# Sparse attention in steps of two items: transposes one step behind, four score buffers, values of two heads on 64 columns each

## The chip, the cores and the metric

The kernel runs on one core of one Trainium2 chip. The metric is the device time of one execution in microseconds (us); three runs of the kernel before gave a median of 2213.21 us, from 2212.78 to 2218.43.

## The reference, cut to what matters

Two transformer blocks follow each other on a sequence of 256 tokens and a width of 1024. The second block has two layers; each mixes tokens by three branches (a convolution, a differential attention, a sparse attention), merges them by gates and adds a feed-forward part. The change lies in the sparse attention (`nsa_attention`) of these two layers: 8 heads of width 64 in two groups that share keys and values. With 256 tokens every block of keys is selected and the window covers all keys, so that both softmax branches are causal attention over 256 keys:

```python
o_cmp = jnp.einsum('bghsn,bngd->bsghd', p_cmp, vc_c)          # 15 compressed keys
o_sel = jnp.einsum('bqghn,bgqnd->bqghd', jax.nn.softmax(sc, axis=-1), vg)
o_win = jnp.einsum('bghqk,bkgd->bqghd', jax.nn.softmax(sc, axis=-1), vwin)
o = g[..., 0:1] * o_cmp + g[..., 1:2] * o_sel + g[..., 2:3] * o_win
...
merged = (gates[:, :, 0] * (y_a @ w_branch[0])
          + gates[:, :, 1] * (y_b @ w_branch[1])
          + gates[:, :, 2] * (y_c @ w_branch[2]))
```

## The kernel before

**Weights.** All weights come as one stream of 572 pieces (128x1024, 512 KB), loaded by SyncE into a ring of seven `raw` buffers. A dense product in about full precision is made of three fast ones: ScalarE rounds a piece to `whi` (L1113, `hi_to`), VectorE (L1721) or GpSimd (L2526) forms the rest `wlo` (`lo_to`), and TensorE adds `whi` times the high part, `whi` times the low part and `wlo` times the high part of the activations (`lin`, L464 to L466). `whi` and `wlo` are rings of five; `hi_to` and `lo_to` run four pieces ahead of their use, and the high part of a piece waits until TensorE has used the piece five before it. A tile of 128 outputs over 1024 inputs takes one piece and 24 products of 256 columns. The `raw` buffer of a piece is free once its low part is made.

**Order.** Every engine has its own function (`tensor`, `scalar`, `vector`, `gpsimd`), and each writes down its instructions in program order, which no scheduler changes. Waits are semaphores that the helper `on(point)` looks up. So a wait in one engine holds everything that stands behind it on that engine. Buffers and PSUM banks are rings: `bank("pm", ...)` hands out five banks in turn, `bank("pt", ...)` two, and `buf(...)` scratch buffers of `tmpb`; each request names the event until which the buffer is held.

**The stretch of the change.** In each layer, after the compressed keys are scored (`c_scores`, `c_turn`), a loop of 18 rounds interleaves the sparse attention with 18 dense tiles, `late(2)` to `late(19)`: the last two `ya` tiles (three pieces each) and 16 `gate` tiles (one piece each). The attention has 16 items, an item being one head and one half of the queries; `pair_item(n)` gives head `2*(n//4)+n%2` and half `(n//2)%2`. An item of half 0 sees 128 keys, one of half 1 sees 256. An item passes:

- `n_scores` (TensorE, L997, for two items at once): both branches, 64 rows of the array for each head;
- `masked` (VectorE, L2184 and L2187): mask, row maximum, its negative; per branch;
- exp with row sum (ScalarE, L1574), per branch;
- reciprocal, gate, scaling of the probabilities (VectorE, L2308, L2310, L2315);
- `n_turn` (TensorE, L1010): transposes, two for half 0 and four for half 1;
- copy of the transposes to `nT` (ScalarE, L1583).

`n_value(h)` (TensorE, L1020 to L1024) then multiplies values by probabilities for one head: compressed (15 rows), and for each branch 256 and 128 columns. The values `VD` and the compressed values `cmp_v` hold the 64 columns of a head twice side by side, so that the result stands on all 128 PSUM partitions; ScalarE (`YCh`, L1594) and VectorE (`YCl`, L2321) take the half that belongs to the head. The second copy in `VD` is made by VectorE (L2171, event `vdc`), and until then the PSUM banks of the values' projection are held.

In round n of the loop TensorE does: scores of n and n+1 if n is even, transposes of n-1, `late(n+2)`, values of the head that n-1 completed, and in four rounds `d_spread` for the other attention. VectorE does `masked(n)`, its part of `late(n+2)` (the low part of a weight piece), then the scaling of item n, then `YCl`. ScalarE does the exp of n, the copy of n-1's transposes, the high part of a piece and the activation of the gate (L1535), then `YCh`. The probabilities lie in a ring of three scratch buffers. After the loop comes the merge: for m in 0 to 7 a tile `mz` and three tiles `mb` (one for each branch, four input tiles each), the third of which reads `YCh` and `YCl`. ScalarE's gate of `mz` (L1616) goes to scratch buffers 3 and 4.

## Time and profile before

| | us |
|---|---|
| median of three runs | 2213.21 |
| lowest, highest | 2212.78, 2218.43 |
| the profiled execution, its time | 2212.25 |
| its span, first to last instruction | 2210.5 |
| TensorE busy | 2026.9 (92%) |
| VectorE busy | 1191.3 (54%) |
| ScalarE busy | 971.3 (44%) |
| GpSimd busy | 456.4 (21%) |
| loop of the change, layer 0: first scores to last values | 1239.2 to 1355.4 |
| the same in layer 1 | 1792.2 to 1904.5 |

Busy time of TensorE includes pipelined overlap, so that its stalls are better read from the waits and from gaps in its order of instructions. The mean granted clock of TensorE over the span is 0.953 of full speed; 1.00 is the level of 2.4 GHz and 0.5 that of 1.2 GHz, and a value between them is a stretch that had some of both.

### The profile page before, as it was taken

How to read it: one execution, taken by the hardware profiler on the slowest of the kernel's cores; microseconds unless marked ns; L12 is line 12 of the kernel's file. 1: busy time of each engine (PE TensorE's matmuls, PEld its weight loads, DVE VectorE, ACT ScalarE, POOL GpSimd, SP SyncE). 2: the span in 40 equal slices, each digit the busy share in tenths (PEclk: the TensorE clock that was granted, in tenths of full speed). 3: DMA queues.
4: the chain of work that ended last, by engine and by line, in shares of the span. 5: the costliest groups of instructions: out<-in, count | busy, mean ns of one | idle time of the engine just before them, and what ended most of it. 6: DMA issues, size and time to landing. Idle time of an engine off the chain costs nothing. (4 is left out here: it accounts for less than half of the span.)

```text
span 2210.5 us, 35650 instructions
## 1 busy us (share of the span) xinstructions
PE 2026.9 (92%) x14700; PEld 1788.8 (81%) x14700; DVE 1191.3 (54%) x2372; ACT 971.3 (44%) x1741; POOL 456.4 (21%) x247
## 2 busy tenths in 40 slices
PE   5999799999987998899998889999989889999997
PEld 2855578888866767799987879999988788899997
DVE  4787443233353554555565545664656555567464
ACT  3314432222333356444445444465544445446564
POOL 1030100000012135000001111435251111253534
PEclk8999899999997999999999999999999989999999
DMA  8234523223232342555533424545543342454551
GB/s 342 96 122 157 190 77 97 94 95 99 98 117 97 107 171 91 190 186 182 181 118 113 142 91 130 172 144 183 185 157 124 108 141 96 134 167 149 185 178 58
DMA packets 84546, 307.48 MB, mean 139 GB/s; under 512 B 9377, under 2 KB 10657, under 8 KB 84001
## 3 DMA queue, kind: packets, MB, share of 16 engines
q1 hardware_dynamic: 84384, 305.20, 41.3%
q8 instruction: 117, 1.92, 0.4%
q14 instruction: 45, 0.36, 0.1%
HBM read 304.12 MB, written 1.05 MB: 138 GB/s over the span
## 5 line engine op out<-in xcount | busy, mean ns | idle before, releaser
L464 PE MATMUL pb<-Hh,whi 128*128 128x256 f32 (+1 forms) x2832 | 890.0, 314 | 45.1 <-DVE Hl L1781 15.0
L465 PE MATMUL pb<-Hl,whi 128*128 128x256 f32 (+1 forms) x2832 | 878.8, 310 | 0.0
L466 PE MATMUL pb<-Hh,wlo 128*128 128x256 f32 (+1 forms) x2832 | 878.2, 310 | 0.0
L1721 DVE TENSOR_TENSOR wlo<-raw,whi 128x1024 fp32r<-128x1024 f32 x325 | 409.7, 1266 | 442.6 <-ACT whi L1113 442.0
L1113 ACT ACTIVATE whi<-raw 128x1024 fp32r<-128x1024 f32 x468 | 488.5, 1053 | 329.1 <-PE pb L466 317.2
L464 PEld LDWEIGHTS pb<-Hh,whi 128*128 128x128 f32 x2832 | 558.2, 197 | 73.8 <-issue 30.6
L465 PEld LDWEIGHTS pb<-Hl,whi 128*128 128x128 f32 x2832 | 558.4, 197 | 22.6
L466 PEld LDWEIGHTS pb<-Hh,wlo 128*128 128x128 f32 x2832 | 557.5, 197 | 23.1
L2526 POOL TENSOR_TENSOR wlo<-raw,whi 128x1024 fp32r<-128x1024 f32 x143 | 344.7, 2423 | 921.5 <-ACT whi L1113 921.5
L2534 POOL TENSOR_TENSOR X<-X,tmpb 128x512 f32<-128x512 f32 (+1 forms) x12 | 16.6, 1384 | 502.2 <-DVE tmpb L1822 502.2
L464 PE MATMUL pb<-hid_h,whi 128*128 128x512 f32 (+1 forms) x352 | 119.2, 339 | 0.0
L465 PE MATMUL pb<-hid_l,whi 128*128 128x512 f32 (+1 forms) x352 | 119.2, 339 | 0.0
L466 PE MATMUL pb<-hid_h,wlo 128*128 128x512 f32 (+1 forms) x352 | 119.2, 339 | 0.0
L464 PE MATMUL pb<-fh,whi 128*128 128x256 f32 x352 | 99.6, 283 | 0.0
L465 PE MATMUL pb<-fl,whi 128*128 128x256 f32 x352 | 99.0, 281 | 0.0
L466 PE MATMUL pb<-fh,wlo 128*128 128x256 f32 x352 | 99.0, 281 | 0.0
L514 PE MATMUL pb<-raw,csz 128*32 128x512 f32 x384 | 60.7, 708 | 26.4 <-DMA raw<-wstream 26.0
L1688 ACT ACTIVATE tmpb<-pb,VEC 128x256 f32<-128x256 f32 x88 | 48.4, 564 | 79.1 <-PE pb L466 79.1
L1867 DVE SCALAR_TENSOR_TENSOR Y<-U,VEC,Y 128x512 f32<-128x512 f32 x120 | 81.8, 755 | 0.0
L1275 ACT ACTIVATE tmpb<-pb 128x512 f32<-128x512 f32 (+1 forms) x44 | 21.6, 491 | 128.7 <-PE pb L466 128.7
L2486 DVE SCALAR_TENSOR_TENSOR tmpb<-pb,VEC,tmpb 128x255 f32<-128x255 f32 x88 | 42.4, 481 | 65.2 <-ACT tmpb L1688 64.1
L464 PEld LDWEIGHTS pb<-hid_h,whi 128*128 128x128 f32 x352 | 66.3, 188 | 8.0
(290 smaller groups left out, 2604.7 us busy)
## 6 DMA issues: line engine op xcount, KB each, us to landing
raw<-wstream SPq DMA_DIRECT2D x572, 512.0 KB, 3.5
X<-xin SPq DMA_DIRECT2D x2, 1024.0 KB, 8.4
CON<-consts SPq DMA_DIRECT2D x1, 1182.0 KB, 9.8
out<-X SPq DMA_DIRECT2D x8, 128.0 KB, 1.7
VEC<-vecs SPq DMA_DIRECT2D x1, 662.0 KB, 10.9
CON<-consts SPq DMA_DIRECT2D x1, 147.0 KB, 5.4
VEC<-vecs SPq DMA_DIRECT2D x1, 88.0 KB, 2.0
```

The source lines that it names most:

```text
L464: e.matmul(dst, hi, xh, start=k == 0, stop=False)
L465: e.matmul(dst, hi, xl, start=False, stop=False)
L466: i = e.matmul(dst, lo, xh, start=False, stop=k == kt - 1)
L514: i = e.matmul(dst[32 * c:32 * c + 32, :], csz[:, 4 * half + c, o:o + 32], raw[:, p % NRAW, (c % 2) * 512:(c % 2 + 1) * 512], start=m == h ...
L1113: e.activation(whi[:, s % NPIECE, :], raw[:, p % NRAW, :], ACT.Copy).then_inc(sig("act_hi", ("hi", p)), 1)
L1275: e.activation(t[:, 0:n], slots.at(("lin", "up", l, j, 0))[:, 0:n], ACT.Silu).then_inc(sig("act_ev", ("ev", "up", l, j, 0)), 1)
L1688: e.activation(t[:, s * T:(s + 1) * T], slots.at(("lin",) + key)[:, 0:T], ACT.Identity, scale=vec("ffn_conv_w_2", l * 132 + 88 + c), bias= ...
L1721: e.tensor_tensor(wlo[:, i, :], raw[:, p % NRAW, :], f32(whi[:, i, :]), ALU.subtract).then_inc(sig("dve_lo", ("lo", p)), 1)
L1867: c = e.scalar_tensor_tensor(out=y, in0=u, scalar=wt, in1=y, op0=ALU.mult, op1=ALU.add)
L2486: e.scalar_tensor_tensor(out=cv[:, 1:T], in0=bk[:, 0:T - 1], scalar=vec("ffn_conv_w_2", c + 44), in1=cv[:, 1:T], op0=ALU.mult, op1=ALU.add ...
L2526: e.tensor_tensor(wlo[:, i, :], raw[:, p % NRAW, :], f32(whi[:, i, :]), ALU.subtract).then_inc(sig("pool_lo", ("lo", p)), 1)
L2534: e.tensor_tensor(xs, xs, two(t) if segs == 2 else t[:, 0:T], ALU.add).then_inc(sig("pool_x", ("x", R, k)), 1)
```

## The change

The loop becomes nine steps of two items. In step P TensorE does the scores of items 2P and 2P+1, `late(2P+2)`, in steps 3, 5 and 7 the values of a pair of heads, the transposes of item 2P-2, `late(2P+3)`, the transposes of item 2P-1, and in steps 5 to 8 `d_spread`. The values of the last pair are computed after the first `mb` tile of the merge. VectorE masks both items of a step, scales item 2P, and scales item 2P+1 after its parts of both `late` tiles. The ring of probabilities gets a fourth buffer (scratch 7), and `nT` is held until the values of the pair. `VD` keeps the 64 columns once, VectorE's second copy and its event are gone, and the two heads of a pair are computed by products of 64 columns of weights, one on PSUM partitions 0 to 63 and one on 64 to 127, in turn. `YCh` and `YCl` are then one instruction for each pair.

```diff
-            scratch(11.5 + 10 * l, p=[0, 1, 2], nT=[3, 4, 5, 6, 9, 10])
+            scratch(11.5 + 10 * l, p=[0, 1, 2, 7], nT=[3, 4, 5, 6, 9, 10])
...
-                        lin_tok(key, "vvg", 280, 2, XS, xon, lambda s: [("vdc", l, s)])
+                        lin_tok(key, "vvg", 280, 2, XS, xon, lambda s: [("vda", l, s)])
...
-                    e.matmul(b[:, 0:T], cmp_v[g], PC[:, h, :], start=True, stop=False)
+                    halves = [(2 * hp + i, b[64 * i:64 * i + 64, 0:T]) for i in range(2)]
+                    for h, y in halves:
+                        e.matmul(y, cmp_v[h // 4][:, 0:64], PC[:, h, :], start=True, stop=False)
                     for br in range(2):
-                        a3 = two(slots.at(("nT", l, h, br)))
-                        e.matmul(b[:, 0:T], VD[:, 0, br, g, :], a3[:, 0, :], start=False, stop=False)
-                        i_ = e.matmul(b[:, 128:T], VD[:, 1, br, g, :], a3[:, 1, 128:T], start=False, stop=br == 1)
-                    i_.then_inc(sig("pe_att", ("no", l, h)), 1)
+                        for h, y in halves:
+                            e.matmul(y, VD[:, 0, br, h // 4, :], two(slots.at(("nT", l, h, br)))[:, 0, :], start=False, stop=False)
+                        for h, y in halves:
+                            i_ = e.matmul(y[:, 128:T], VD[:, 1, br, h // 4, :], two(slots.at(("nT", l, h, br)))[:, 1, 128:T],
+                                          start=False, stop=br == 1)
+                    i_.then_inc(sig("pe_att", ("no", l, hp)), 1)
...
-                for n in range(18):
-                    if n < 16 and n % 2 == 0:
-                        n_scores(n)
-                    if 0 <= n - 1 < 16:
-                        n_turn(n - 1)
-                    late(n + 2)
-                    if 0 <= n - 1 < 16 and pair_item(n - 1)[1]:
-                        n_value(pair_item(n - 1)[0])
...
+                for P in range(9):
+                    if P < 8:
+                        n_scores(2 * P)
+                    late(2 * P + 2)
+                    if P in (3, 5, 7):
+                        n_values((P - 3) // 2)
+                    if P:
+                        n_turn(2 * P - 2)
+                    late(2 * P + 3)
+                    if P:
+                        n_turn(2 * P - 1)
+                    if P > 4:
+                        d_spread(P - 5)
...
                         lin([("mb", l, m, br)], 4, src, T, xo)
+                        if m == br == 0:
+                            n_values(3)
...
+                for P in range(9):
+                    if P < 8:
+                        n_exp(2 * P)
+                    hi_to(("ya", l, 2, 0) if P == 0 else ("gate", l, LATE[2 * P + 2][1]))
+                    if P < 8:
+                        n_exp(2 * P + 1)
+                    late(2 * P + 2)
...
+                    if P in (3, 5, 7):
+                        yc_hi((P - 3) // 2)
+                    if P:
+                        n_out(2 * P - 2)
+                    late(2 * P + 3)
...
+                    if P:
+                        n_out(2 * P - 1)
...
-                            e.tensor_copy(VD[:, s, :, :, 64:128], b4).then_inc(sig("dve_cmp", ("vdc", l, s)), 1)
...
+                for P in range(9):
+                    if P < 8:
+                        n_masked(2 * P)
+                        n_masked(2 * P + 1)
+                    if P < 8:
+                        n_scaled(2 * P)
+                    late(2 * P + 2)
...
+                    if P in (3, 5, 7):
+                        yc_lo((P - 3) // 2)
+                    late(2 * P + 3)
...
+                    if P < 8:
+                        n_scaled(2 * P + 1)
```

TensorE at the values of the first heads, layer 0. Before, the values of head 0, then the next scores and the transposes of item 3, right before the next gate tile:

```order
L1020 MATMUL pb<-Y,MOD 128x256 [waits act_att,dve_ya]
L1023 MATMUL pb<-tmpb,VD 128x256
L1024 MATMUL pb<-tmpb,VD 128x128
L997 MATMUL pb<-KD,NQ 128x128 [waits dve_att]
L997 MATMUL pb<-KD,NQ 128x128 x3
L1010 MATMUL pb<-CON,tmpb 128x128 [waits dve_att]
L1010 MATMUL pb<-CON,tmpb 128x128 x3
L464 MATMUL pb<-Hh,whi 128x256 [waits dve_lo,act_ev]
```

Now, in step 3, the values of heads 0 and 1, two for two, and behind them the transposes of item 4, whose scores stood in step 2:

```order
L1022 MATMUL pb<-Y,MOD 64x256 [waits act_att,act_ev]
L1022 MATMUL pb<-Y,MOD 64x256
L1025 MATMUL pb<-tmpb,VD 64x256 x2
L1027 MATMUL pb<-tmpb,VD 64x128 x2
L1010 MATMUL pb<-CON,tmpb 128x128 [waits dve_att]
L1010 MATMUL pb<-CON,tmpb 128x128
L464 MATMUL pb<-Hh,whi 128x256 [waits dve_lo,act_ev]
```

(In both, the rows of the second branch, which repeat the first, are left away.) Ten products of 128 columns of weights for two heads have become ten of 64 columns, and what a transpose follows is no longer the scores of its own round.

ScalarE at the end of the loop and the first tile of the merge, layer 0. Before:

```order
L1535 ACTIVATE Y<-pb 128x256 [waits pe_lin]
L1594 ACTIVATE YCh<-pb 64x256 [waits pe_att]
L1599 ACTIVATE Hh<-DQ 128x256 [waits dve_ya]
L1113 ACTIVATE whi<-raw 128x1024 [waits raw_landed2]
L1535 ACTIVATE Y<-pb 128x256 [waits pe_lin]
L1113 ACTIVATE whi<-raw 128x1024 [waits raw_landed3]
L1616 ACTIVATE tmpb<-pb 128x256 [waits pe_lin]
L1113 ACTIVATE whi<-raw 128x1024 [waits raw_landed4]
```

Now:

```order
L1544 ACTIVATE Y<-pb 128x256 [waits pe_lin]
L1593 ACTIVATE tmpb<-pb 128x2x128 [waits pe_att]
L1593 ACTIVATE tmpb<-pb 128x2x128
L1622 ACTIVATE Hh<-DQ 128x256 [waits dve_ya]
L1122 ACTIVATE whi<-raw 128x1024 [waits raw_landed3]
L1639 ACTIVATE tmpb<-pb 128x256 [waits pe_lin,pe_att]
L1122 ACTIVATE whi<-raw 128x1024 [waits raw_landed4]
L1600 ACTIVATE YCh<-pb 128x256
```

The gate of `mz` (L1616, now L1639) has gained a wait for `pe_att`: its scratch buffer 3 holds `nT` of head 6 until the values of the last pair, which TensorE now computes after the first `mb` tile; `YCh` of that pair comes one piece later.

## Rows read from the trace of the kernel before

**Rows 1.** Page: span, and each engine's busy us (share) xinstructions.

```profile
span 2210.5 us, 35650 instructions
PE 2026.9 (92%) x14700; PEld 1788.8 (81%) x14700; DVE 1191.3 (54%) x2372; ACT 971.3 (44%) x1741; POOL 456.4 (21%) x247
```

**Rows 2.** Waits of TensorE: line waited by, for whom, us in total, times, longest.

```profile
PE pb L1010 <- DVE tmpb L2315: 32.7, 14, 5.1
PE pb L464 <- DVE VD L2171: 3.6, 2, 2.4
```

**Rows 3.** Timeline, rounds 6 and 7, layer 0: start us, us, [idle before <- releaser].

```profile
1287.79 1.13 PE L997 MATMUL pb<-KD,NQ 64*128 64x256 f32 x8
1288.86 0.44 PE L1010 MATMUL pb<-CON,tmpb 128*128 128x128 f32 x2
1289.06 0.42 DVE L2184 CUSTOM_DVE_ANT_0 tmpb<-pb,CON 128x256 f32<-128x256 f32 x1 [1.06 <-PE pb L997]
...
1290.76 0.43 ACT L1583 ACTIVATE tmpb<-pb 128x128 f32<-128x128 f32 x2
1291.07 1.06 ACT L1113 ACTIVATE whi<-raw 128x1024 fp32r<-128x1024 f32 x1
1292.16 1.23 DVE L1721 TENSOR_TENSOR wlo<-raw,whi 128x1024 fp32r<-128x1024 f32 x1 [1.95 <-ACT whi L1113]
1293.70 0.62 DVE L2315 TENSOR_SCALAR tmpb<-tmpb,SM 128x256 f32<-128x256 f32 x2
1294.46 0.41 PE L1010 MATMUL pb<-CON,tmpb 128*128 128x128 f32 x2 [2.29 <-DVE tmpb L2315]
```

**Rows 4.** Stretches of dense products: us, PE busy (x), PEclk, DMA share, GB/s.

```profile
1239.80:1248.70 8.90, 8.90 (x74) 1.00 0.18 58
1254.10:1264.40 10.30, 10.30 (x74) 0.83 0.45 144
1289.00:1292.10 3.10, 3.10 (x26) 1.00 0.01 1
1294.80:1299.40 4.60, 4.60 (x28) 0.63 0.25 97
```

**Rows 5.** Timeline of TensorE, values of head 0, layer 0, to the next scores.

```profile
1276.34 0.69 PE L1020 MATMUL pb<-Y,MOD 15*128 15x256 f32 x2
1276.96 0.70 PE L1023 MATMUL pb<-tmpb,VD 128*128 128x256 f32 x2
1277.50 0.38 PE L1024 MATMUL pb<-tmpb,VD 128*128 128x128 f32 x2
1277.72 0.60 PE L1023 MATMUL pb<-tmpb,VD 128*128 128x256 f32 x2
1278.15 0.39 PE L1024 MATMUL pb<-tmpb,VD 128*128 128x128 f32 x2
1278.47 0.38 PE L997 MATMUL pb<-KD,NQ 64*128 64x128 f32 x2
```

**Rows 6.** Timeline of TensorE, products on 32 columns; their line's loads, ns min/median/max.

```profile
19.45 1.07 PE L514 MATMUL pb<-raw,csz 128*32 128x512 f32 x8 [0.75 <-DMA raw<-wstream]
20.31 0.32 PE L554 MATMUL pb<-tmpb,CON 128*32 128x128 f32 x4
...
L514 PEld LDWEIGHTS pb<-raw,csz x384: 104/110/178, 6.2 to 896.1; 128*32 128x32 f32 x192
```

**Rows 7.** Timeline of VectorE, end of the values' projection, layer 0, and TensorE's next waits.

```profile
1178.29 2.81 DVE L1721 TENSOR_TENSOR wlo<-raw,whi 128x1024 fp32r<-128x1024 f32 x1 [0.48 <-ACT whi L1113]
1181.02 0.41 DVE L2171 COPY VD<-pb 128x256 f32<-128x256 f32 x1
...
1185.46 0.58 PE L546 MATMUL pb<-CON,tmpb 128*128 128x1 f32 x4 [0.72 <-ACT tmpb L1494]
```

**Rows 8.** Groups in the loop of layer 0: busy us, mean ns, idle before.

```profile
L1721 DVE TENSOR_TENSOR wlo<-raw,whi 128x1024 fp32r<-128x1024 f32 x14 | 18.2, 1303 | 29.9 <-ACT whi L1113 29.9
L1113 ACT ACTIVATE whi<-raw 128x1024 fp32r<-128x1024 f32 x21 | 22.1, 1055 | 1.6 <-PE pb L466 1.6
L1594 ACT ACTIVATE YCh<-pb 64x256 fp32r<-64x256 f32 x7 | 2.6, 378 | 12.2 <-PE pb L1024 12.2
```

**Rows 9.** Stretch of the loop, layer 0: us, PE, PEld, DVE, ACT, POOL busy, PEclk, DMA share, GB/s.

```profile
1239.20:1361.10 121.90, 105.04 (x760) 96.80 (x760) 59.49 (x206) 61.08 (x158) 19.06 (x8) 0.93 0.30 96
```

More of the change, by code:

```diff
@@ L1050, in tensor @@
                         else:
-                            src, xo = (lambda k: (YCh[:, k, :], YCl[:, k, :])), (lambda k: [("ycl", l, 2 * k), ("ycl", l, 2 * k + 1)])
+                            src, xo = (lambda k: (YCh[:, k, :], YCl[:, k, :])), (lambda k: [("ycl", l, k)])
                         lin([("mb", l, m, br)], 4, src, T, xo)
+                        if m == br == 0:
+                            n_values(3)
                 def centered(F, keys, kt, src, xo):
@@ new lines, in n_exp @@
+                def n_exp(n):
+                    nk = 128 * (pair_item(n)[1] + 1)
+                    p, sm = slots.at(("np", l, n)), slots.at(("nsm", l, n))
+                    for br in range(2):
+                        w.wait_ge(*on("nneg", l, n, br))
+                        pb = p[:, br * 256:br * 256 + nk]
+                        e.activation(pb, pb, ACT.Exp, bias=sm[:, 4 * br + 1:4 * br + 2], scale=SC,
+                                     accum_out=sm[:, 4 * br + 2:4 * br + 3]).then_inc(sig("act_att", ("nexp", l, n, br)), 1)
@@ new lines, in n_out @@
+                def n_out(n):
+                    h, qt = pair_item(n)
+                    if qt == 0:
+                        for br in range(2):
+                            for u in slots.take(st + 1.5, "nT", ("nT", l, h, br), ("no", l, h // 2)):
+                                w.wait_ge(*u)
+                    w.wait_ge(*on("nt", l, n))
+                    for br in range(2):
+                        i = e.activation(two(slots.at(("nT", l, h, br)))[:, 0:qt + 1, qt * 128:(qt + 1) * 128],
+                                         slots.at(("nt", l, n))[:, br * 256:br * 256 + 128 * (qt + 1)].rearrange(
+                                             "p (s q) -> p s q", q=128), ACT.Copy)
+                    i.then_inc(sig("act_att", ("nte", l, n)), 1)
@@ L1624, in scalar @@
                         hi_to(("mb", l, m, br))
+                        if m == br == 0:
+                            yc_hi(3)
                 merged(7)
@@ new lines, in n_masked @@
+                def n_masked(n):
+                    qt = pair_item(n)[1]
+                    nk = 128 * (qt + 1)
+                    p = buf(st + 1.5, "p", ("np", l, n), ("nt", l, n))
+                    sm = buf(0, "small", ("nsm", l, n), ("nn", l, n))
+                    w.wait_ge(*on("ns", l, n))
+                    for br in range(2):
+                        masked(slots.at(("ns", l, n))[:, br * 256:br * 256 + nk], nk, qt, p[:, br * 256:br * 256 + nk],
+                               sm[:, 4 * br:4 * br + 4], [("nmask", l, n)] if br else [], ("nneg", l, n, br))
@@ new lines, in n_scaled @@
+                def n_scaled(n):
+                    h, qt = pair_item(n)
+                    nk = 128 * (qt + 1)
+                    p, sm = slots.at(("np", l, n)), slots.at(("nsm", l, n))
+                    w.wait_ge(*on("nexp", l, n, 1))
+                    e.reciprocal(sm[:, 8:10], sm[:, 2:7:4]).then_inc(sig("dve_att", ("nrec", l, n)), 1)
+                    w.wait_ge(*on("nrec", l, n))
+                    e.tensor_tensor(sm[:, 10:12], sm[:, 8:10], gate3[:, qt, 3 * h + 1:3 * h + 3], ALU.mult).then_inc(
+                        sig("dve_att", ("ngate", l, n)), 1)
+                    w.wait_ge(*on("ngate", l, n))
+                    for br in range(2):
+                        pb = p[:, br * 256:br * 256 + nk]
+                        i = e.tensor_scalar(pb, pb, sm[:, 10 + br:11 + br], None, ALU.mult)
+                    i.then_inc(sig("dve_att", ("nn", l, n)), 1)
@@ new lines, in yc_lo @@
+                def yc_lo(hp):
+                    w.wait_ge(*on("ych", l, hp))
+                    e.tensor_tensor(YCl[:, hp, :], slots.at(("no", l, hp))[:, 0:T], f32(YCh[:, hp, :]), ALU.subtract).then_inc(
+                        sig("dve_ya", ("ycl", l, hp)), 1)
+                for P in range(9):
[5 more added lines that the diff above has]
+                    late(2 * P + 2)
+                    if P == 0:
+                        ya_lo(2, slots.at(("fa", l, 2))[:, 0:T])
+                    if P in (3, 5, 7):
+                        yc_lo((P - 3) // 2)
+                    late(2 * P + 3)
+                    if P == 0:
+                        ya_lo(3, slots.at(("fa", l, 3))[:, 0:T])
+                    if P < 8:
+                        n_scaled(2 * P + 1)
+                    if P > 5:
+                        ya_lo(P - 2, DQ[:, P - 6, :])
+                    if P > 4:
+                        w.wait_ge(*on("spread", ("d", l, P - 5)))
+                        e.scalar_tensor_tensor(out=DQ[:, P - 5, :], in0=DQ[:, P - 5, :], scalar=subln,
+                                               in1=slots.at(("spread", ("d", l, P - 5)))[:, 0:T],
+                                               op0=ALU.mult, op1=ALU.mult).then_inc(sig("dve_ya", ("dnorm", l, P - 5)), 1)
@@ L2333, in merged_lo @@
+                ya_lo(7, DQ[:, 3, :])
                 def merged_lo(k):
@@ L2344, in vector @@
                         lo_to(key)
+                        if m == br == 0:
+                            yc_lo(3)
                         gt = gate_at(8 * br + m) if br < 2 else slots.at(("g2", l, m))[:, 0:T]
```

96 lines of the change are left out of this document (16 added, 80 removed).

## The prediction

> **What bounds the kernel now.** The page first: TensorE is busy for 92% of the span, VectorE for 54%, ScalarE for 44% [rows 1]. So the end is set by TensorE, and the question of the change is where TensorE stands still, and what it does that it need not do. TensorE's list of waits answers the first part: its longest entry is the transpose of the sparse attention (L1010) behind VectorE's scaling (L2315), 32.7 us in 14 waits [rows 2]. They all lie in the two loops that the change rewrites. For the loop of layer 0 the windows give 105.04 us of TensorE in 121.9, thus 16.9 idle [rows 9], and the waits of that layer come to the same.
>
> The timeline shows why it waits. TensorE computes the scores of items 6 and 7 from 1287.79 and a gate tile to 1292.17, and can transpose item 6 only at 1294.46 [rows 3]. Between lie VectorE's mask (1289.06), ScalarE's exp, its copy of older transposes (1290.76), its high part of a weight piece (1291.07 to 1292.13), VectorE's low part of that piece (1292.16 to 1293.39) and only then the scaling (to 1294.32). The scaling stands behind the low part, the low part waits for the high part, and that stands behind the exp. The whole is 6.7 us, and TensorE has one round of work, some 4.4 us, to put beside it. No engine is full: they are in a ring, and the ring is shorter than its latency.
>
> A wait has an after-effect in the granted clock. Seventy-two dense products take 8.9 us at a clock of 1.00, and 10.3 us at 0.83 right behind the longest wait; twenty-four take 3.1 at 1.00 and 4.6 at 0.63 right behind a wait of 2.3 [rows 4]. These means are mixtures of the two levels, 1.2 and 2.4 GHz. Before each fall TensorE had stood still.
>
> **The change, part by part.** The sum is made against the profiled execution's own 2212.25 us, which is 1.0 below the median of the three runs shown.
>
> *Waits of the transposes.* A transpose of item 2P now stands a whole step behind its scores. A step of TensorE is scores (1.07 for two items of 256 keys [rows 3], less for 128), two tiles of 3.1 [rows 4] and two sets of transposes of some 0.2 to 0.4: 7.6 us at least. From the scores to the transpose of item 2P there are then that step, the next scores and a tile, 11 us or more, and 14 for item 2P+1. Against this: masks of two items (0.54 for each branch, from 1289.06 to 1289.60 [rows 3], so 2.2), the exp of some 1.1 for both branches, the scaling of 1.0 for item 2P, in all under 5; for item 2P+1 another high part of 1.06, two low parts of 1.3 [rows 8] and the scaling, in all under 10. Both fit with 4 us or more to spare, so I let all 32.7 us go.
>
> *The clock behind them.* In six of the 14 places the tiles behind ran slow: two times 1.4 (72 products) and four times 1.5 (24 products) [rows 4]: 8.8 us. No gap, no fall: -8.8.
>
> *Values on 64 columns.* A head costs 2.13 us (1276.34 to 1278.47) [rows 5]. From the same rows, a product of 256 columns takes 0.43 (1277.72 to 1278.15), one of 128 takes 0.22 (1277.50 to 1277.72): three and two of them are 1.73, and 0.40 is start and exposed weight loads. Sixteen heads are 34.1 us. Now two heads go together, half of the array's columns each. Whether the halves run at the same time the loop before doesn't show; the nearest row is L514, with 32 columns: eight instructions, which are four products of 512 columns on four column groups, start at 19.45 and the next line starts at 20.31 [rows 6]. That is 0.86 us for four, the time that one product of 512 columns takes by rows 5 (two times 0.43). So column groups overlap fully. For a pair the lower bound is 1.73, the upper one is no overlap and every load bare: 3.46 plus 20 loads of 0.11 [rows 6], 5.7. I take 1.73 plus the 0.40 of today plus 0.2 for entering and leaving another division of the array, 2.3, near the lower end because L514 is the same kind of product. Eight pairs are 18.4: -15.7, with bounds of -20.3 and +11.
>
> The Trainium skill (TensorE: Matmul & The Clock Gate, Part 3) speaks against this: it has weight loads overlap with running products only where the row groups differ, and the halves share all row groups. L514's groups share them too, and show no such cost in their 0.86 us; that rule's case is the second rival.
>
> *VectorE's second copy of the values.* TensorE waited 3.6 us in two places for it [rows 2], because it stood behind a low part that took 2.81 beside GpSimd [rows 7]. That wait goes, but not its whole price: TensorE next waits at L546 for ScalarE's square (0.72) [rows 7], whose chain starts on VectorE behind the same low part and moves up only by the two removed copies, 0.82. So 0.8 in layer 0 and some 1.3 in layer 1, whose wait was the longer: -2.1, with bounds of 0 and -5 (all of it and a slow tile).
>
> *Banks, buffers, the merge.* The fourth buffer of probabilities was the scratch of `ya` tile 2 and is free before item 3. The gate of the first `mz` on ScalarE now waits for the values of the last pair, which TensorE computes behind `mz` and an `mb` tile. ScalarE stands there some 6 us with four weight pieces, 12 us of TensorE, made ahead. After the values it does the gate (0.38), a high part (1.06) and `YCh` (0.38), then VectorE `YCl` (0.42): 2.2 us. TensorE has the second `mb` tile (1.5) and three of four inputs of the third (1.1) before it needs them, 2.6. I cost it at nothing; if the cover were 1 us short, it would be 2 us for both layers. Half of the `YCh` and `YCl` instructions go from engines that nobody waits for: nothing. The stream of weights: 96 GB/s in the loop [rows 9], a quarter faster after it, and 144 in a stretch of it [rows 4]: nothing.
>
> Sum: 2212.25 - 32.7 - 8.8 - 15.7 - 2.1 = 2152.95, and with the 1.0 to the median **2154 us**, 2.7% faster.
>
> **Rivals.**
>
> *Second: the halves don't overlap, or their loads stand bare.* A pair then costs 3.46 plus the 0.4 to 0.8 of starts, or 1.73 plus 20 loads of 0.11 plus some start, both about 4.1, as today. For it: a load of 64 columns has to happen between two products of the same half. Against it: L514. The time is 2154 + 8 x 1.8 = 2168.
>
> *Third: waits come back in another place.* For it: a low part took 2.81 instead of 1.23 where GpSimd worked beside it [rows 7], ScalarE and VectorE stand at `YCh` and `YCl` until the values are done (12.2 us before ScalarE's seven copies in layer 0 [rows 8]), and both keep strict order. Against it: of the new stretch, 121.9 less 16.9, 5.8 and 7.9, thus 91 us, VectorE's 59.5 and ScalarE's 61.1 us [rows 9] are two thirds. If half of the waits and slow tiles stay, it is 2154 + 20.7 = 2175.
>
> *Fourth, slower: the chain of a step does not fit into the next one.* ScalarE has the copy of item 2P-1's transposes, the last thing of TensorE's step, ahead of the next exp. If the exp starts so late that every scaling misses its transpose, all 32 transposes wait, not 14. At the 2.3 us of rows 3, with 1.5 us of slow clock in each of 16 steps, that is 98 us, and 2252 us. It decides against the change from a mean wait of 1.4 us on each transpose and those slow tiles, which use up the 59 us gained. Against it: the copy ends half a microsecond into the next step, and the exp's mask is ready only after 1.5 us.
>
> *Fifth: no change.* The wait of the transposes only showed the ring of weight pieces, and TensorE stands in front of its dense tiles instead, for the same time and with the same slow clock, the values saved being waited away too: 2213. Against it: no dense tile of the loop waited for a weight piece [rows 2, 8]; VectorE waited for ScalarE's high part (29.9 us) while TensorE was not waiting for VectorE's low part.
>
> **How the numbers follow.** Forecast 0.70, second 0.11, third 0.13, fourth 0.03, fifth 0.03. The range: below 2154 lie the bounds of the values (4.6), of the copy (3) and gaps whose hidden tail also goes, not all at once: 2146. Above, it takes in the second rival and the third as a whole: 2176. This leaves out the fourth and the fifth and ends below. Measured differences of 0.3%, 6.6 us, are about what can be told from no change for this kernel. The first three cases are faster than that, the fifth is the same: faster 0.94, same 0.03, slower 0.03.
>
> **What the profile of the changed kernel would show.** The entry L1010 behind VectorE's scaling gone from TensorE's waits, or under 2 us; no new entry there above 3 us in the two loops. A granted clock of 1.00 in both loops, and 0.96 to 0.97 over the span. From the first row of a pair's values to the next line 2.3 us; 4.1 would be the second rival. VD gone from the waits, and L546 waiting for ScalarE in both layers. `YCl` not among the waits of the merge. The loop of layer 0 in about 84 us instead of 116, its last values now behind it. Wrong would be the forecast if a dense tile (L464) or a set of transposes waits for VectorE or ScalarE in more than a few steps, which would show as gaps of 1 to 5 us with slow tiles behind them.

## The result, and the profile after

The changed kernel takes 2158.13 us (median of four runs, 2153.48 to 2165.93) against 2215.82 in the runs of the kernel before beside it: a ratio of 0.974, 95% interval 0.970 to 0.978, thus 2.6% faster. Its profiled execution took 2153.48, the one before 2212.25: 58.8 us less.

The page, span and busy times, to set beside [rows 1]:

```profile
span 2151.7 us, 35658 instructions
PE 2002.1 (93%) x14700; PEld 1767.0 (82%) x14700; DVE 1185.4 (55%) x2360; ACT 966.2 (45%) x1733; POOL 458.2 (21%) x247
```

TensorE's waits, to set beside [rows 2] (line waited by, for whom, us in total, times, longest):

```profile
PE pb L514 <- DMA raw<-wstream: 20.8, 10, 6.6
PE pb L546 <- ACT tmpb L1503: 3.7, 2, 2.2
PE pb L464 <- DVE YCl L2343: 0.8, 2, 0.4
```

L1010, with its 32.7 us, is no longer in the list at all. VD is gone, and L546 behind ScalarE has taken almost all of its place (3.7, before 0.7). `YCl` is new.

To compare kernels, take the stretch from the first sparse scores (L997) of a layer to the first product of the merge that reads `YCh`. It holds the same work in every kernel here: the attention, 18 tiles, one `mz` and two `mb` tiles, the values of all heads. I call it the loop stretch. Before, both layers (us, PE, PEld, DVE, ACT, POOL busy, PEclk, DMA share, GB/s):

```profile
1239.20:1364.10 124.90, 108.04 (x785) 99.80 (x785) 61.19 (x208) 62.40 (x160) 19.06 (x8) 0.93 0.31 99
1792.20:1913.24 121.04, 105.20 (x785) 96.93 (x785) 60.78 (x208) 62.39 (x160) 19.02 (x8) 0.96 0.32 103
```

and after, both layers:

```profile
1234.60:1327.70 93.10, 93.10 (x786) 86.11 (x785) 56.36 (x201) 59.37 (x156) 19.51 (x8) 1.00 0.42 138
1756.10:1849.20 93.10, 93.10 (x786) 86.13 (x786) 59.41 (x201) 59.55 (x156) 19.44 (x8) 1.00 0.42 137
```

In the changed kernel TensorE stands still in neither layer, and the clock is granted in full. Before, the two took 124.9 and 121.0, together 245.9; now 186.2. In the two stretches of before the clock was granted at 1.2 GHz in six places, 27.3 us in all, and TensorE was busy for 21.5 of them. The weights come at 138 GB/s now, before at 99, and no product in the stretch waits for them. The whole balance of the two profiled executions is then: loop stretches -59.7; all ahead of the first one -4.6 (1239.2 to 1234.6, with L514's waits for DMA 5.2 shorter); between them +0.3; behind the second +5.2. The sum is -58.8.

How far a transpose now stands from its scores, TensorE and VectorE, layer 0:

```profile
1277.29 0.71 PE L997 MATMUL pb<-KD,NQ 64*128 64x128 f32 x8
1280.12 0.48 DVE L2338 TENSOR_SCALAR tmpb<-tmpb,SM 128x128 f32<-128x128 f32 x2
1284.70 0.48 DVE L2338 TENSOR_SCALAR tmpb<-tmpb,SM 128x128 f32<-128x128 f32 x2
1290.90 0.44 PE L1010 MATMUL pb<-CON,tmpb 128*128 128x128 f32 x2
1294.05 0.38 PE L1010 MATMUL pb<-CON,tmpb 128*128 128x128 f32 x2
```

The scores of 1277.29 are scaled by 1280.6 and 1285.2 and transposed at 1290.90 and 1294.05: 9 to 10 us are to spare, where the transposes of [rows 3] waited 2.29. But this is the middle of the loop. The least is near its start, at item 3 of layer 0 (its scaling, and the transposes that read it):

```profile
1264.99 0.62 DVE L2338 TENSOR_SCALAR tmpb<-tmpb,SM 128x256 f32<-128x256 f32 x2
1267.14 0.60 PE L1010 MATMUL pb<-CON,tmpb 128*128 128x128 f32 x4
```

Between the end of the scaling, 1265.6, and the transposes lie 1.5 us. Items 1 and 2 have 1.6 and 2.5 there, the same three items of layer 1 have 2.2, 3.1 and 4.3, and every other item has 5.9 or more. In VectorE's order the scaling of item 1 stands behind its parts of both `ya` tiles, three weight pieces each, and items 2 and 3 stand behind that.

### The profile page after: what moved, and what is told of

Same layout as the page of the kernel before. It is cut to its first block, busy times and chain, and to the rows that moved or that the text cites. A ratio compares the mean times of both kernels' runs of the same rounds, so it can differ in the third digit from the quotient of the medians.

```text
span 2151.7 us, 35658 instructions
## 1 busy us (share of the span) xinstructions
PE 2002.1 (93%) x14700; PEld 1767.0 (82%) x14700; DVE 1185.4 (55%) x2360; ACT 966.2 (45%) x1733; POOL 458.2 (21%) x247
## 4 chain that ended last, share of the span: by engine, by line
PE 84%; DVE 9%; ACT 4%; DMA 1%; issue 1%; POOL 0%; ACTq 0%; SPq 0%; DVEq 0%
PE pb L464 24%; PE pb L465 23%; PE pb L466 23%; DVE Y L1892 2%; DVE wlo L1746 1%; DMA raw<-wstream 1%; PE pb L514 1%; ACT whi L1122 1%; DVE tmpb L2435 1%; PE pb L722 1%; PE pb L782 1%; PE pb L864 1%; PE pb L571 1%; PE pb L997 1%; PE pb L1010 1%
## 5 line engine op out<-in xcount | busy, mean ns | idle before, releaser
L514 PE MATMUL pb<-raw,csz 128*32 128x512 f32 x384 | 60.6, 708 | 21.2 <-DMA raw<-wstream 20.8
L466 PEld LDWEIGHTS pb<-hid_h,wlo 128*128 128x128 f32 x352 | 66.2, 188 | 8.0
```

The costliest lines, as they stand in the source:

```text
L466: i = e.matmul(dst, lo, xh, start=False, stop=k == kt - 1)
L514: i = e.matmul(dst[32 * c:32 * c + 32, :], csz[:, 4 * half + c, o:o + 32], raw[:, p % NRAW, (c % 2) * 512:(c % 2 + 1) * 512], start=m == h ...
```

## The experiments

Times are medians with the lowest and highest run; the ratio is to the kernel before in the same job (medians 2213.78, 2212.88, 2213.92 and 2216.46). "Loops" is the sum of the two loop stretches in the profile.

| kernel | median us | ratio, 95% interval | loops us |
|---|---|---|---|
| before | 2215.82 | 1 | 245.9 |
| lag alone | 2196.12 (2189.77-2201.23) | 0.992 (0.989-0.995) | 224.7 |
| pair values alone | 2203.27 (2199.36-2212.79) | 0.995 (0.993-0.997) | 232.3 |
| lag and pair values, rounds of one | 2186.99 (2185.11-2191.33) | 0.989 (0.985-0.992) | 212.6 |
| steps of two, values close | 2171.13 (2167.83-2178.45) | 0.982 (0.978-0.986) | 198.3 |
| changed | 2158.13, again 2161.45 | 0.974, 0.975 (0.972-0.977) | 186.2, 186.2 |
| changed, no lag | 2185.03 (2182.06-2188.36) | 0.987 (0.984-0.990) | 214.4 |
| changed, 128-column values | 2181.37 (2176.59-2184.26) | 0.985 (0.982-0.988) | 202.7 |
| changed, halves in turn | 2180.77 (2175.20-2184.69) | 0.984 (0.981-0.988) | 202.1 |
| changed, three buffers | 2158.57 (2151.14-2165.63) | 0.973 (0.969-0.978) | 186.3 |
| changed, copy put back | 2155.28 (2151.74-2161.63) | 0.973 (0.970-0.977) | 186.1 |
| changed, gates moved | 2161.93, again 2157.37 | 0.975, 0.974 (0.972-0.977) | 186.1, 186.1 |

**The lag alone.** The kernel before with transposes, copies and values one item further behind, and the fourth buffer:

```diff
-                    if 0 <= n - 1 < 16:
-                        n_turn(n - 1)
+                    if 0 <= n - 2 < 16:
+                        n_turn(n - 2)
```

> The kernel before, with the transposes (and all that follows them) two items behind the scores instead of one, and the fourth buffer; rounds, values on 128 columns and the second copy as before. If the lateness of the scaling was all that the transposes waited for, the 32.7 us of waits at L1010 and the 8.8 us of slow tiles go: about 2171 us on the profiled run, 0.981 of before. If the grouping in steps of two was needed as well, waits of 10 us or more stay at L1010: 2185 or more.

The loops lost 21.2 us, not 41.5. Neither half of the expectation fits: the time is that of the second, 2185 or more, but the waits that it names, at L1010, are not there. L1010's wait for the scaling is down to 0.8 us, as it should be, but two waits have come in (TensorE's waits of this kernel):

```profile
PE pb L1020 <- ACT tmpb L1583: 7.7, 4, 3.1
PE pb L464 <- DVE SM L2184: 5.2, 3, 2.7
```

The values wait for ScalarE's copy of the transposes, although a dense tile lies between, and a dense tile waits for VectorE's mask, until which the scores hold a PSUM bank. This is my third rival, in a kernel that has only a part of the change.

**The pair's values alone.** The kernel before with 64-column values and no second copy, its lag of one item kept:

```diff
-                    if 0 <= n - 1 < 16 and pair_item(n - 1)[1]:
-                        n_value(pair_item(n - 1)[0])
+                    if 0 <= n - 1 < 16 and n % 4 == 0:
+                        n_values(n // 4 - 1)
```

> The kernel before, with the values of a pair of heads on 64 columns each and without the second copy; rounds and lag as before. If the terms simply add, 17 to 19 us go: 2195. If the ring of mask, exp, weight piece and scaling sets the pace of the loop (four rounds in 23.0 us), the values were hidden beside it and TensorE waits longer at its transposes instead: L1010 waits of 40 us or more, and a gain of 2 to 6 us only, 2206 to 2210.

The loops lost 13.6 us, so the gain lies between the two expectations. A part of what TensorE saved it stood waiting, with three more waits and 2.4 us more than in [rows 2], and not the 40 us or more of the second:

```profile
PE pb L1010 <- DVE tmpb L2314: 35.1, 17, 5.1
```

**Values on 128 columns in the changed kernel** (two banks for a pair, VectorE's second copy back):

```diff
-                    halves = [(2 * hp + i, b[64 * i:64 * i + 64, 0:T]) for i in range(2)]
-                    for h, y in halves:
-                        e.matmul(y, cmp_v[h // 4][:, 0:64], PC[:, h, :], start=True, stop=False)
+                    for i in range(2):
+                        h, y = 2 * hp + i, bs[i][:, 0:T]
+                        e.matmul(y, cmp_v[h // 4], PC[:, h, :], start=True, stop=False)
```

> The kernel after, with the values of each head on 128 columns again, one head after the other in two banks, and with the second copy and its wait. If TensorE is now the bound of the loops, the whole difference of the values comes back, 8 times 4.26 less 2.03 us, 17.8, and 1 us for the copy: 19 us above the kernel after, about 2172 on a run like its profiled one. If something else paces the loops, less than 8 us.

The loops grew by 16.5 us, about the 17.8 expected. A pair took 4.17 us (1277.93 to 1282.10) in place of 2.03. The median is 23 us above the changed kernel's, where 19 were expected, and so is the profiled span. Of these 23, 6.1 us lie ahead of the first scores (1240.8 against 1234.6), where the same code differs from profile to profile (below).

**The changed kernel without the lag**, transposes in the step of their scores. The values of a pair then stand in steps 2, 4, 6 and 8 (the lines shown are those of the transposes):

```diff
-                    if P:
-                        n_turn(2 * P - 2)
+                    if P < 8:
+                        n_turn(2 * P)
```

> The kernel after, with the transposes of items 2P and 2P+1 in step P itself, behind the first and the second dense tile, and the values in steps 2, 4, 6 and 8. If the lag of a step is what removes the waits, they come back as before, 25 us or more at L1010 with slow tiles, 2185 or more. If the order of a step (both masks first, scaling of item 2P ahead of the weight pieces) does most of it, by the durations only items 2P+1 of odd steps wait, some 1 us each: 5 to 12 us of waits, 2160 to 2166.

```profile
PE pb L1010 <- DVE tmpb L2334: 19.3, 11, 5.7
```

The loops grew by 28.2 us, of which 19.3 are this wait (and 1.5 for ScalarE). A part of the rest is slow clock: right behind the wait of 5.69 us the eight products of the next scores took 2.08 us, in [rows 3] 1.13. TensorE was busy for 10.1 us at 1.2 GHz in the two loops, which costs half of that, 5.0; the last 2.4 us are not accounted for. The time is that of the first expectation, but the waits lie between the two: the order in steps takes 13.4 of the 32.7 us away without the lag. The lag is the largest single edit: 21.2 us as the first part; as the last 28.2, together with the values' other place.

**Halves in turn.** The five products of one head, then the five of the other, same shapes and same columns:

```diff
                     for h, y in halves:
                         e.matmul(y, cmp_v[h // 4][:, 0:64], PC[:, h, :], start=True, stop=False)
-                    for br in range(2):
-                        for h, y in halves:
+                        for br in range(2):
```

> The changed kernel with one edit: of a pair's ten products the five of the first head come first, then the five of the second, in place of one and one. The shapes, the columns used and the waits stay. If the two halves of the array run beside each other only because neighbours in the queue use different halves, a pair goes from the 2.03 us of the changed kernel's trace (1271.80 to 1273.83) to 3.5 to 4.1: 1.73 for each head, or the 4.1 of my second rival. Eight pairs are then 12 to 16 us, and the time 2170 to 2174. If it is enough that both are in the queue, or if a product of 64 columns is cheaper for another reason, a pair stays at 2.0 to 2.5 and the time within 4 us of the changed kernel's.

TensorE's timeline of a pair in the changed kernel, to the next transposes:

```profile
1271.80 0.65 PE L1022 MATMUL pb<-Y,MOD 15*64 15x256 f32 x4
1272.38 0.65 PE L1025 MATMUL pb<-tmpb,VD 128*64 128x256 f32 x4
1272.86 0.39 PE L1027 MATMUL pb<-tmpb,VD 128*64 128x128 f32 x4
1273.08 0.60 PE L1025 MATMUL pb<-tmpb,VD 128*64 128x256 f32 x4
1273.51 0.39 PE L1027 MATMUL pb<-tmpb,VD 128*64 128x128 f32 x4
1273.83 0.44 PE L1010 MATMUL pb<-CON,tmpb 128*128 128x128 f32 x2
```

and with the halves in turn, the first head and the start of the second:

```profile
1278.05 0.64 PE L1022 MATMUL pb<-Y,MOD 15*64 15x256 f32 x2
1278.62 0.65 PE L1024 MATMUL pb<-tmpb,VD 128*64 128x256 f32 x2
1279.10 0.38 PE L1025 MATMUL pb<-tmpb,VD 128*64 128x128 f32 x2
1279.32 0.59 PE L1024 MATMUL pb<-tmpb,VD 128*64 128x256 f32 x2
1279.75 0.38 PE L1025 MATMUL pb<-tmpb,VD 128*64 128x128 f32 x2
1280.07 0.64 PE L1022 MATMUL pb<-Y,MOD 15*64 15x256 f32 x2
```

A product is two instructions here, each with its weight load. Each row of the first view has four instructions in the time in which the second has two. A pair goes from 2.03 to 4.03 us (1278.05 to 1282.08), and the loops grow by 15.9, eight times 2.0. The gain of the shape comes from the alternation: a product of 64 columns is hardly cheaper than one of 128 (a head takes 2.02 here, 2.13 in [rows 5]), and no product of the second head starts ahead of the first head's. It isn't the loads that alternation hides. They are hidden with the halves in turn as well. Weight loads of this kernel, the first head's:

```profile
1278.62 0.19 PEld L1024 LDWEIGHTS pb<-tmpb,VD 128*64 128x64 f32 x2 [0.38 <-issue]
1278.89 0.35 PEld L1025 LDWEIGHTS pb<-tmpb,VD 128*64 128x64 f32 x2
```

The first load starts with its own product; the next ones run beside products of the same half, which last from 1278.62 to 1279.27. What alternation gains is that the products of the two halves run side by side.

The time is not the 2170 to 2174 expected but 2180.77: in the profile, 6.3 us more than in the changed kernel's stand ahead of the first scores, 5.6 between the two loop stretches, and 1.4 fewer behind the second.

**Three buffers** of probabilities in the changed kernel:

```diff
-            scratch(11.5 + 10 * l, p=[0, 1, 2, 7], nT=[3, 4, 5, 6, 9, 10])
+            scratch(11.5 + 10 * l, p=[0, 1, 2], nT=[3, 4, 5, 6, 9, 10])
```

> The changed kernel with three buffers of probabilities in place of four. The masks of item n then wait until item n-3 has been transposed: those of 2P+1 for the transpose of 2P-2, which TensorE does in the same step behind a dense tile. Theory A (there is slack enough): from that transpose to the one of 2P+1 are a dense tile, another step's scores, a tile and a set, 10 us or more, against masks, exp and scaling of about 3.5; the time stays within 4 us of the changed kernel's and no wait on VectorE's scaling over 1 us returns. Theory B (the fourth buffer is what makes the lag work): the waiting masks hold VectorE's low parts behind them, as it keeps strict order, so dense tiles (L464) or transposes (L1010) wait, 1 to 2.3 us in most of eight steps of two loops, with slow tiles: 2175 to 2200.

Theory A. The loops are the same to 0.1 us, and no wait for the scaling came back. In this order the fourth buffer does nothing.

**The copy put back** (VectorE writes the values once more, and TensorE waits for it):

```diff
+                            e.tensor_copy(VD[:, s, :, :, :], slots.at(("lin", key, s))[:, 0:256].rearrange(
+                                "p (b g d) -> p b g d", b=2, g=2)).then_inc(sig("dve_cmp", ("vdc", l, s)), 1)
```

> The changed kernel with VectorE's second copy of the values put back (it writes again what ScalarE wrote), and the values waiting for it. My sum had 2.1 us for the copy. If that holds: a wait of about 1.2 us on VD in each layer in TensorE's list, the wait of L546 on ScalarE falls from 3.7 in two places to 0.7 in one, and the profiled time is 0 to 3 us above the changed kernel's. If the copy costs nothing because L546 waits for the same chain anyway: VD and L546 together come to the 3.7 us of now. If it costs more, up to 5, a further slow tile stands behind the wait. The runs' times alone can't tell these apart; the waits can.

```profile
PE pb L464 <- DVE VD L2195: 3.6, 2, 2.4
...
PE pb L546 <- ACT tmpb L1503: 0.7, 1, 0.7
```

VD and L546 come to 4.3 us with the copy and to 3.7 without it. In the waits the copy is worth 0.6 us, less than any run can tell. Whether a slow tile hangs on it stays open: between the two loop stretches, where the second of these waits lies, this profile took 433.4 us and the changed kernel's 428.4, but kernels without the copy have 433 to 434 there too (values close, halves in turn).

**The gates' scratch moved** to buffers that the attention leaves earlier, so that ScalarE's first gate of the merge doesn't wait for the last values:

```diff
-            scratch(12 + 10 * l, mg=[0, 1, 2], g2=[3, 4])
+            scratch(12 + 10 * l, mg=[0, 1, 2], g2=[9, 10])
```

> The changed kernel with the two scratch buffers of the merge's gates moved to numbers 9 and 10, which the attention leaves earlier, so that ScalarE's first gate need not wait for the values of the last pair. Its only trace in the changed kernel is TensorE's wait of 0.40 us in each layer for the last YCl. My theory: ScalarE does the gate and its high parts ahead, YCh and YCl come some 0.4 to 0.8 us sooner, both waits go, 0.8 us in all, which the runs' times can't tell from nothing. Rival: the gate is held by something else (its own accumulator or the order of VectorE), and the waits stay at 0.3 to 0.5 each.

Both waits for `YCl` went, as expected, and 914.1 us from the first scores to the end stood against 917.1. To settle it, both kernels ran again in one job:

> The changed kernel as it is, once more, beside the one with the gates' scratch moved. From the first sparse scores of layer 0 to the end its profile should have 917 us within 1, as it had (917.1), and so had the kernels with three buffers (916.7) and with the copy put back (917.3). The start before these scores, which no part of the change touches, was 1232.6 to 1250.6 us in the profiles so far: if that is what spreads the runs over 2151 to 2166, a longer profile of this kernel has its excess there and nowhere else.

> The changed kernel with the gates' scratch moved, once more and in the same job as the changed kernel itself, to settle whether it is the better version. From the first sparse scores to the end its first profile had 914.1 against 917.1, with both waits for YCl gone. If that is real: 914 to 915 again, 2 to 3 us below the changed kernel's, and a median lower by 0 to 3, which 5 rounds can hardly tell. If it is an accident of the clock: 916 to 918 for both and no order in the medians.

From the first scores to the end the changed kernel had 917.0, the one with the gates moved 917.0 as well. Its waits for `YCl` are gone in both profiles, and the time is not lower: medians 2161.93 and 2157.37 against 2158.13 and 2161.45. No version here beats the changed kernel measurably. The second expectation, that a longer profile has all its excess ahead of the first scores, came true: 2158.7 against 2151.7 us of span, and 1241.7 against 1234.6 at the scores.

**Lag and pair values, rounds of one item.** The two parts together, in the order of the kernel before:

```diff
-                        n_turn(n - 1)
+                        n_turn(n - 2)
...
-                    if 0 <= n - 1 < 16 and pair_item(n - 1)[1]:
-                        n_value(pair_item(n - 1)[0])
+                    if 0 <= n - 2 < 16 and n % 4 == 1:
+                        n_values(n // 4 - 1)
```

> The kernel before with three parts of the change and without the fourth: transposes two items behind, four buffers, the 64-column values of a pair; but in rounds of one item, and the values right behind the round that made the last transposes. Counted from the first sparse scores of layer 0 to the end, which leaves out the start, the profiles so far give 971.3 us before, 955.3 with the lag alone, 960.6 with the pair's values alone, 917.1 with the whole change: 16.0 and 10.7 apart, 54.2 together, so 27.5 us belong to neither part alone. Theory A (lag and 64 columns help each other: each hides in the other's wait): this kernel has most of the 27.5 us, thus 917 to 925, a time of 2158 to 2168, and no waits over 1 us in the loops. Theory B (the order in steps with the values a scores and a tile later is what is missing): the waits of the lag alone remain, values on ScalarE's copy 7.7 us and dense tiles on the mask 5.2 us, each with slow tiles behind; 971.3 less 26.7, about 945, a time near 2185.

Theory B, in size (2186.99, and 947.3 us from the first scores to the end) and in the waits:

```profile
PE pb L1021 <- ACT tmpb L1586: 9.7, 6, 3.2
PE pb L464 <- DVE SM L2183: 5.0, 2, 2.7
PE pb L1010 <- DVE tmpb L2314: 2.4, 3, 1.2
```

The 27.5 us that belong to neither part alone are not something that the two parts give each other. In the loops they gave 21.2 and 13.6 alone and 33.3 together, and from the first scores to the end 16.0 and 10.7 alone and 24.0 together: by either sum they about add up. What is left belongs to the order in steps, 26.4 us in the loops. The timeline shows how rounds of one item make the wait (VectorE, ScalarE, TensorE, layer 0):

```profile
1281.47 1.23 DVE L1722 TENSOR_TENSOR wlo<-raw,whi 128x1024 fp32r<-128x1024 f32 x1 [2.05 <-ACT whi L1116]
1283.40 0.29 DVE L2183 CUSTOM_DVE_ANT_0 tmpb<-pb,CON 128x128 f32<-128x128 f32 x1
1283.92 0.40 ACT L1577 ACTIVATE tmpb<-tmpb,SM 128x128 f32<-128x128 f32 x1 [2.21 <-DVE SM L2186]
1284.71 0.64 ACT L1586 ACTIVATE tmpb<-pb 128x256 f32<-128x256 f32 x2
1285.49 1.12 PE L1021 MATMUL pb<-Y,MOD 15*64 15x256 f32 x4 [3.21 <-ACT tmpb L1586]
```

The scores of two items are made together (1272.03), but the odd one is masked only a round later, behind a low part (1281.47) and a scaling. ScalarE stands 2.21 us in front of its exp, with the copy of older transposes behind it, and for that copy TensorE waits 3.21, although a dense tile stands between these transposes and the values. A step of two masks both items ahead of the low parts.

**Steps of two, values close.** The changed kernel, a pair's values right behind its last transposes. The last pair's values move from the merge into step 8:

```diff
-                    if P in (3, 5, 7):
-                        n_values((P - 3) // 2)
...
+                    if P in (2, 4, 6, 8):
+                        n_values(P // 2 - 1)
```

> The changed kernel with a pair's values moved back to the end of the step that makes its last transposes, ahead of the next scores, so that ScalarE's copy of these transposes lies bare. The rest of the order in steps stays. From the first sparse scores to the end the changed kernel has 917.1 us. If the place of the values matters as I think: eight waits for ScalarE's copy of 0.7 to 2 us and slow tiles behind each (1.5 us for one or two tiles), together 12 to 28 us, thus 929 to 945, a time of 2170 to 2186. Rival: ScalarE stands ready by then, the copy takes 0.6 us, the clock doesn't fall after so short a wait: 5 us, 922 and 2163.

The loops grew by 12.1 us, and the time, 2171.13, is in the range expected. There were eight waits, 9.4 us in all; two of them in layer 0 (TensorE):

```profile
1272.14 1.11 PE L1022 MATMUL pb<-Y,MOD 15*64 15x256 f32 x4 [3.60 <-ACT tmpb L1591]
...
1292.56 0.65 PE L1022 MATMUL pb<-Y,MOD 15*64 15x256 f32 x4 [0.84 <-ACT tmpb L1591]
```

Behind 3.60 us of standing still the same four products took 1.11 us, behind 0.84 they took their usual 0.65. Here the seven waits of 0.75 to 0.98 us cost themselves, and the long one a slow stretch too. The length of a wait alone doesn't decide it: of the 14 waits in the loops before, six were followed by a stretch at 1.2 GHz, the shortest of them 1.78 us long, while one of 3.32 us was not (behind it, from 1272.91, the clock is 1.00).

## Why the prediction was right, and where not

The forecast was 2154 us and the change came out at 2158.13, by the mechanism forecast: the waits and the slow clock behind them went, and the values of two heads run side by side. That it is as near as 4 us is in part luck, as the last item says. Step by step, in the loops:

- *Waits of the transposes, -32.7.* Right: not one is left. The durations behind it were not right everywhere: 4 us or more to spare were forecast, and items 1 to 3 had 1.5 to 2.5 in layer 0 and 2.2 to 4.3 in layer 1, the others 5.9 or more. The forecast had costed a step of gate tiles, not the first one with its `ya` tiles. And the reason in the text, the distance between scores and transposes, is only a part of it. With the distance alone the loops gained 21.2 of the 41.5 us of waits and slow clock. The rest needs VectorE's and ScalarE's order within a step. The chain before, step by step, is 245.9 to 224.7 (lag), to 212.6 (pair values), to 198.3 (steps of two), to 186.2 (values behind the next scores and a tile). The last two, 26.4 us, I had never costed; they are what keeps the third rival away, which I gave 0.13 on the ground of both engines' free time. The argument of free time didn't bear on it: in the rounds of one item the engines are as free, and the waits came.
- *The clock behind them, -8.8.* Right in kind: the clock is 1.00 in both loop stretches. As a remainder it is 59.7 less 32.7 and 17.8, thus 9.2. From the clock itself: TensorE was busy for 21.5 us at 1.2 GHz in the loops before, and at 2.4 GHz the same work would take half, which makes 10.7. The 8.8 is a little small by both.
- *Values, -15.7.* Undersized by 2.1: a pair took 2.03 us, not 2.3, so 8 times 4.26 less 2.03 is 17.8. The 0.2 for entering and leaving another division of the array was not there, nor any other surcharge. The second rival is the kernel with halves in turn: its pair took 4.03, for which I had said 4.1. Of its two premises, halves that don't overlap and bare loads, the first is what this kernel shows, and the order of the products makes it; the loads are hidden there too.
- *VectorE's second copy, -2.1.* Wrong: 0.6. The step that failed is that L546's chain "moves up by the two removed copies, 0.82". L546's wait grew from 0.7 to 3.7, so it takes nearly all that VD gave.
- *The merge, 0.* Wrong by 0.8. I had 2.2 us from the last values to `YCl`, and 2.6 of cover. In the trace `YCl` ends at 1329.28, 3.1 us after the next products began at 1326.18: ahead of it VectorE has a low part of 1.22 (1327.73) that I had left out, since it could not be made before ScalarE's high part.
- *The fourth buffer.* I took it as needed and free; in the changed order it is free and not needed.
- *The rest of the kernel, 0.* The profile has -4.6 ahead of the loops and +5.2 behind. Neither was forecast. Here they cancel, and so the sum of 2152.95 for the profiled execution fits its 2153.48 better than its terms do: the loops gave 59.7 for 57.2. That is luck. The forecast had the stream of weights a quarter faster; 99 to 138 GB/s is more, since a stretch that is a quarter shorter has to bring the same weights at a rate a third higher. It cost nothing.

What the profile was to show: L1010 gone, clock 1.00 in the loops and 0.959 over the span (0.96 to 0.97 had been said), L546 waiting for ScalarE in two places, the loop of layer 0 at 85 us (1234.64 to 1319.66, where the `mz` tile begins) for 84. Only `YCl` stood against it. One sum of the fourth rival was wrong without effect on the rest: with 24 us of slow clock, the 59 us gained are used up by a mean wait of 1.1 us on each of 32 transposes, not 1.4.

## What to carry over

When a transpose waits for a chain through two other engines, moving it further back is half of the work. The other half here was order: both items' first operations ahead of the long independent ones on every engine of the chain, and the consumer of a copy behind the next scores and a dense tile. Right behind the transposes it waited, up to 3.6 us; with one dense tile between, but in rounds of one item, up to 3.2. Two products that use different column halves have to stand alternately in the program, or nothing is gained. And compare variants by a stretch that holds the same work: outside it two profiles of one and the same kernel were up to 16 us apart, and the lag's 21.2 us in the loops were 16.0 from the first scores to the end.

## What the runs showed of the hardware

Two column halves of the array, with all rows in common, run side by side: ten products, which one half after the other took 4.03 us, took 2.03 in alternation. The products of one half take 1.73 us of it, so that the twenty weight loads can stand bare for 0.30 us at most. By the rule of the Trainium skill (TensorE: Matmul & The Clock Gate, Part 3) loads overlap with running products only where row groups differ; the measurement decides against it, for two column halves and, by the loads shown for the halves in turn, within one half as well. The Trainium skill's page TensorEngine Tiling (Array Packing), section Tiling Modes, has tiles load and multiply independently, and with that the trace agrees. The drain that the same section gives for a change of tiling mode has to fit into the same 0.30 us, with all starts.

Outside the loops the profiles differ where nothing was edited. Ahead of the loops, where the kernels with 64-column values do the same work (one has a copy more), their first scores come anywhere from 1232.6 (copy put back) to 1250.6 us (gates moved). Two profiles of one kernel can be as far apart: with the gates moved it was 1250.6 and 1234.5. A stretch of it in the changed kernel, where TensorE is busy throughout:

```profile
775.00:800.00 25.00, 25.00 (x156) 17.31 (x155) 15.44 (x43) 13.79 (x34) 8.91 (x8) 0.93 0.46 167
```

and in the one with three buffers, at a lower granted clock and with 133 products for 156:

```profile
775.00:800.00 25.00, 25.00 (x133) 17.72 (x132) 12.92 (x34) 10.03 (x25) 8.45 (x6) 0.77 0.37 134
```

And behind the loops, from `YCh` to the end, the changed kernel needs 302.5 us where the one before needed 297.3. At the same distance behind `YCh`, 80 to 100 us, it has

```profile
1929.19:1939.19 10.00, 7.54 (x44) 6.75 (x43) 4.90 (x10) 4.61 (x9) 1.14 (x2) 0.67 0.47 157
1939.19:1949.19 10.00, 9.02 (x54) 9.05 (x55) 7.82 (x20) 5.28 (x10) 7.02 (x9) 0.67 0.01 2
```

against, before,

```profile
1993.24:2003.24 10.00, 6.46 (x36) 5.74 (x36) 6.59 (x15) 4.34 (x8) 1.10 (x2) 0.67 0.51 157
2003.24:2013.24 10.00, 10.00 (x79) 10.00 (x78) 8.49 (x17) 5.86 (x9) 7.26 (x8) 0.91 0.01 2
```

Nearly the same waits are followed by a longer stretch at the lower level. The second profile of the changed kernel repeats this to 0.1 us (302.4), though it came there 7 us later, and the two with the gates moved have 299.0 both. Between the loops it is otherwise: the changed kernel has 428.4 twice, but with the gates moved it is 429.0 in one profile and 431.8 in the other. So where the waits and the work of a stage are the same, the share of it that runs slow can still differ, from kernel to kernel and at times from run to run. What sets it is open; no run here was made for it.
